# Gathering the experts' rows in quarters and turning them on VectorE, in a decoder layer with a mixture of experts

## What is computed

```python
def moe_ffn(hn, w_router, b_router, w_gate_up, b_gate_up, w_down, b_down):
    logits = (xt @ w_router).astype(jnp.float32) + b_router.astype(jnp.float32)
    top_vals, top_idx = lax.top_k(logits, TOP_K)
    gates = jax.nn.softmax(top_vals, axis=-1)
    ...
    xs = xt[tok]
    h = lax.ragged_dot(xs, w_gate_up, group_sizes) + b_gate_up[e_sorted]
    glu = jnp.minimum(h[:, ::2], SWIGLU_LIMIT)
    lin = jnp.clip(h[:, 1::2], -SWIGLU_LIMIT, SWIGLU_LIMIT)
    act = glu * jax.nn.sigmoid(SWIGLU_ALPHA * glu) * (lin + 1.0)
    y = lax.ragged_dot(act, w_down, group_sizes) + b_down[e_sorted]
    y = y * gates.reshape(-1)[order].astype(y.dtype)[:, None]
    out = jax.ops.segment_sum(y, tok, num_segments=T)
```

## Time and profile before

| | |
|---|---|
| median of 3 runs | 2709.56 us (2707.67 to 2709.72) |
| span of the profiled execution | 2705.4 us |
| instructions | 49571 |
| granted TensorE clock | 0.9 of full speed or more in 38 of 40 slices, 0.8 in two |
| DMA queue q1 (weights, all of SyncE's) | 498.99 MB, 50.2% of 16 engines |

### The profile page before, as it was taken

How to read it: one execution, slowest core, us unless ns; L and a number is a source line. 1 busy time by engine, 2 the same in 40 slices (tenths; PEclk the granted TensorE clock), 3 DMA queues, 4 the chain that set the end, 5 groups by cost and what they waited for, 6 DMA issues and landing times.

```text
span 2705.4 us, 49571 instructions
## 1 busy us (share of the span) xinstructions
PE 2638.0 (98%) x17206; PEld 2118.7 (78%) x17207; DVE 1091.5 (40%) x2701; ACT 627.4 (23%) x1386; POOL 379.9 (14%) x391
## 2 busy tenths in 40 slices
PE   9999999999999998999999999999999999999997
PEld 8455556666477774999999999998878787878785
DVE  1111145554212324433333344344455454545455
ACT  0333355553011112011111111111212121221212
POOL 0100022221000001111111111111111111112111
PEclk9999999999999998999999999999999999999998
DMA  8111243232300002765667677787888888888885
GB/s 293 47 51 54 64 151 90 79 116 92 129 1 9 31 31 103 303 209 194 221 218 254 225 276 260 269 274 264 318 299 319 301 310 306 312 297 312 300 310 202
DMA packets 108856, 533.95 MB, mean 197 GB/s; under 512 B 24290, under 2 KB 59042, under 8 KB 84208
## 3 DMA queue, kind: packets, MB, share of 16 engines
q1 hardware_dynamic: 88016, 498.99, 50.2%
q0 software_dynamic: 20768, 33.97, 5.7%
HBM read 506.64 MB, written 60.52 MB: 210 GB/s over the span
## 4 chain that ended last, share of the span: by engine, by line
PE 92%; DVE 3%; issue 2%; DMA 2%; ACT 1%; DVEq 1%; POOL 0%; ACTq 0%; POOLq 0%
PE bank L1376 45%; PE wide L1376 9%; PE wide L1836 9%; PE wide L1804 9%; PE bank L1426 8%; PE bank L1369 4%; PE wide L1500 2%; PE bank L1556 2%; PE bank L1760 2%; PE wide L1517 1%; DMA d_sum<-y_sb,sidx 1%; PE wide L1369 1%; DVE biased L2060 1%; DVE prob_t L2071 1%; ACT prob L1151 0%
## 5 line engine op out<-in xcount | busy, mean ns | idle before, releaser
L1376 PE MATMUL bank<-xe_t,slot 128*128 128x128 f32 (+4 forms) x8192 | 1025.2, 287 | 12.3 <-issue 11.2
L1376 PEld LDWEIGHTS bank<-xe_t,slot 128*128 128x128 f32 x8192 | 1014.5, 192 | 14.1 <-issue 13.7
L2336 DVE TENSOR_SCALAR glu<-bank,b_gu 128x256 f32<-128x256 f32 x256 | 123.8, 484 | 657.2 <-PE bank L1376 657.1
L1317 ACT ACTIVATE sig<-glu 128x256 f32<-128x256 f32 x256 | 106.7, 417 | 837.8 <-DVE glu L2336 835.5
L1836 PE MATMUL wide<-slot,act_t 128*128 128x512 f32 x608 | 267.8, 593 | 1.0 <-DVE act_t L2348 1.0
L1804 PE MATMUL wide<-act_t,slot 128*128 128x144 f32 (+3 forms) x1664 | 235.5, 302 | 0.0
L1804 PEld LDWEIGHTS wide<-act_t,slot 128*128 128x128 f32 x1664 | 231.8, 190 | 0.0
L1426 PE MATMUL bank<-w_in,xt 128*128 128x512 f32 (+1 forms) x512 | 217.6, 575 | 1.6 <-DVEq L1978 1.6
L1836 PEld LDWEIGHTS wide<-slot,act_t 128*128 128x128 f32 x608 | 112.5, 190 | 128.8 <-issue 126.2
L1334 ACT ACTIVATE y_t<-wide,b_dn 128x256 f32<-128x256 f32 x248 | 102.0, 471 | 421.2 <-PE wide L1836 212.9
L955 POOL DMA_INDIRECT xg<-d_xn,gidx x66 | 66.6, 1009 | 862.8 <-DVE gidx L2290 814.0
(11 more groups left out here) (302 smaller groups left out, 2455.6 us busy)
## 6 DMA issues: line engine op xcount, KB each, us to landing
slot<-in_w_gu SPq DMA_DIRECT2D x128, 2048.0 KB, 8.8
slot<-in_w_dn SPq DMA_DIRECT2D x64, 2048.0 KB, 7.7
w_in<-in_w_in SPq DMA_DIRECT2D x1, 6144.0 KB, 25.3
w_mem_k<-in_w_mem_kv SPq DMA_DIRECT2D x4, 1024.0 KB, 11.0
w_mem_v<-in_w_mem_kv SPq DMA_DIRECT2D x1, 4096.0 KB, 20.6
x_sb<-in_x SPq DMA_DIRECT2D x8, 512.0 KB, 3.3
cneg<-d_cneg SPq DMA_DIRECT2D x8, 512.0 KB, 6.6
d_vw<-mix_out SPq DMA_DIRECT2D x16, 256.0 KB, 2.2
```

The source lines that it names most:

```text
L1317: ac.activation(sig[m % 2][:, :], glu[m % 2][:, :], ACT.Sigmoid, scale=1.702).then_inc(e_sig, 1)
L1376: m = pe.matmul(dst, l, r_, start=(k == 0), stop=(k == n - 1))
L2336: ve.tensor_scalar(glu[b][:, :], pp[b][:, 0:CAP], b_gu[:, bass.ds(e * 2 * KD + 2 * m, 1)], 7.0, ALU.add, ALU.min).then_inc(e_glu, 1)
```

## The change

The gathered rows come to VectorE in such a form that two transposes of 32 x 32 blocks each finish the job, and TensorE turns rows only for the first expert.

- The normed rows are also written to a second table, `d_xq`, with the gain multiplied in (GpSimd, `r_gain`, one product of 128 x 1024 a tile) and each row cut into four interleaved quarters of 1 KB: quarter q holds features 32q to 32q + 31 of each 128. SyncE stores it (`store_quarters`). There is one buffer, `rq`, for all tiles. The gain is brought into row form through a small table `d_g`.
- For every expert but the first, eight indirect DMAs of 128 quarters each replace the two of rows. Partition group q (32 partitions) fetches quarter q, and gather g of a half brings tokens 32g to 32g + 31. The token numbers reach all four partition groups by one more small product (`e_spread`, two bf16 matmuls of 8 columns, after m = 3), and VectorE turns them into indices after its m = 3 (`spread_indices`).
- VectorE's `rows_turned` waits for each half's four gathers and writes `xe_t` directly.
- In GpSimd's queue the scatter of expert i - 1 is issued ahead of the gathers; the wait for its landing and the count in `e_left` stay behind them.
- The one-hots of the first expert and the first weight load wait until the last quarter has been stored.

Cut to its core:

```diff
+        xg_q = nc.alloc_sbuf_tensor_at("xg_q", [P, 2, G32, KD * 32], F32, offset=r.at - 2 * D * 4)
...
+        g_row = Region(59, 63)("g_row", [P, D])
+        rq = Region(55, 59)("rq", [P, G32, KD, 32])
...
+        d_xq = scratch("d_xq", [T * G32, D // G32])
+        d_g = scratch("d_g", [1, D])
...
+            sp.dma_start(d_g[0, :].rearrange("(k p) -> k p", k=KD), a["gains"][:, 3 * KD:4 * KD].rearrange("p k -> k p"),
+                         allow_slow_non_contiguous=True).then_inc(g_row_in, 16)
             sp.wait_ge(c_sum, 1)
+            sp.wait_ge(g_row_in, g_row_in_done + 16)
+            load(g_row[:, :], d_g[0].partition_broadcast(P), g_row_in)
             load(w_xq[:, :, :], rows(a["w_xq"][0]), ld["w_xq"])
...
+            def store_quarters(t):
+                sp.wait_ge(r_rq, r_rq_done + t + 1)
+                sp.dma_start(d_xq[t * P * G32:(t + 1) * P * G32, :].rearrange("(p q) c -> p (q c)", q=G32),
+                             rq.rearrange("p q k d -> p (q k d)")).then_inc(r_stq, 16)
...
             for t in range(NT):
                 if t >= 2:
                     store_rows(t - 2)
+                if t >= 3:
+                    store_quarters(t - 3)
                 if t == NT - 1:
                     store_rows(NT - 2)
+                    store_quarters(NT - 3)
                 sp.wait_ge(x_h, t + 1)
                 if t == NT - 1:
                     store_rows(NT - 1)
+                    for u in range(NT - 2, NT):
+                        store_quarters(u)
                 sp.dma_start(d_sum[t * P:(t + 1) * P, :], h_res[:, t, :]).then_inc(s_st, 16)
...
             sp.wait_ge(r_st, 16 * NT)
+            sp.wait_ge(r_stq, r_stq_done + 16 * NT)
...
+            def r_gain(i):
+                po.wait_ge(r_rn, i + 1)
+                po.wait_ge(r_stq, r_stq_done + 16 * i)
+                apart(po)
+                po.tensor_tensor(rq.rearrange("p q k d -> p k q d"),
+                                 rn[:, bass.ds(i, 1), :].rearrange("p o (k q d) -> p (o k) q d", k=KD, q=G32),
+                                 g_row.rearrange("p (k q d) -> p k q d", k=KD, q=G32), ALU.mult).then_inc(r_rq, 1)
...
                 r_power(i - 1)
+                r_gain(i - 2)
             for t in range(NT - 2, NT):
                 r_rows(t - 2)
                 r_power(t - 1)
+                r_gain(t - 2)
             r_rows(NT - 2)
+            r_gain(NT - 2)
             r_power(NT - 1)
+            r_gain(NT - 1)
...
+            def gather(i):
+                po.wait_ge(e_idx, i + 1)
+                apart(po)
+                for hb in range(2):
+                    for g in range(G32):
+                        n = hb * G32 + g
+                        po.indirect_dma_start(
+                            out=xg_q[:, hb, g, :], out_offset=None, in_=d_xq,
+                            in_offset=bass.IndirectOffsetOnAxis(ap=gidx[:, n:n + 1], axis=0),
+                            bounds_check=T * G32 - 1, oob_is_err=False).then_inc(e_xg[hb], 16)
...
+            def scattered(i):
                 po.wait_ge(e_y.free, 32 * (i + 1))
                 po.sem_inc(e_left, 1)
...
             with po.Fori(1, E) as i:
                 shares(i - 1)
+                scatter(i - 1)
                 gather(i + 1)
-                scatter(i - 1)
+                scattered(i - 1)
...
+            def e_spread(i):
+                pe.wait_ge(e_pt[0].free, spread_use(i))
+                product(pt[0][:, 8:8 + 2 * G32],
+                        [(spread_r.rearrange("p q d -> p (q d)"), ixm[:, c, :, :].rearrange("p h g -> p (h g)"))
+                         for c in range(2)]).then_inc(e_pt[0].full, 1)
...
-                e_gate_up(i, 3, 8, w)
-                e_turn_in(i + 1, (0, 1), later)
+                e_gate_up(i, 3, 4, w)
+                e_spread(i + 1)
+                e_gate_up(i, 4, 8, w)
                 if w == P:
-                    e_rows_down(i, lambda: e_turn_in(i + 1, (2, 3), later))
+                    e_rows_down(i)
                     look_ahead()
                     return
                 e_down_first(i, w)
-                e_turn_in(i + 1, (2, 3), later)
...
+            ve.tensor_reduce(group_r[:, :], ident.rearrange("p (g d) -> p g d", g=G32), AX, ALU.add)
+            ve.tensor_reduce(col_r[:, :], ident.rearrange("p (g d) -> p d g", g=G32), AX, ALU.add)
+            ve.drain()
+            ve.tensor_copy(spread_r[:, :, :], col_r[:, :].unsqueeze(1).to_broadcast([P, G32, 32]))
+            ve.tensor_scalar(quarter_w[:, 0:1], group_r[:, 2:3], 2.0, group_r[:, 1:2], ALU.mult, ALU.add)
+            ve.drain()
+            ve.tensor_scalar(quarter_w[:, 1:2], group_r[:, 3:4], 3.0, quarter_w[:, 0:1], ALU.mult, ALU.add)
+            ve.drain()
+            ve.tensor_scalar(quarter_r[:, :], quarter_w[:, 1:2], float(8 * T * G32), None, ALU.add)
...
+                if not first_one:
+                    x = ve.tensor_tensor(ixm[:, :, :, :],
+                                         pt[0][:, 0:4].rearrange("p (h c) -> p c h", h=2).unsqueeze(3)
+                                         .to_broadcast([P, 2, 2, G32]),
+                                         group_r[:, :].unsqueeze(1).unsqueeze(1).to_broadcast([P, 2, 2, G32]), ALU.mult)
+                x.then_inc(e_pt[0].free, 1)
                 ve.drain()
...
+            def spread_indices(i):
+                ve.wait_ge(e_pt[0].full, spread_use(i))
+                ve.tensor_scalar(gidx[:, :], pt[0][:, 8:8 + 2 * G32], float(G32), quarter_r[:, :], ALU.mult, ALU.add)\
+                    .then_inc(e_pt[0].free, 1)
+                ve.drain().then_inc(e_idx, 1)
...
+            def rows_turned(i):
+                for hb in range(2):
+                    ve.wait_ge(e_xg[hb], rows_landed(i))
+                    ve.transpose(xe_t[:, :, hb * P:(hb + 1) * P].rearrange("p k (g t) -> p k g t", g=G32),
+                                 xg_q[:, hb, :, :].rearrange("p g (k d) -> p k g d", k=KD))
+                ve.drain().then_inc(e_xt, 1)
...
+            ve.wait_ge(r_stq, r_stq_done + 16 * NT)
             hots(0, first)
...
                     if m == 1:
                         indices(i + 1, follow)
+                    if m == 3:
+                        spread_indices(i + 1)
...
-                if last:
-                    x_copies(i + 1, (0, 1))
-                else:
-                    x_copies(i + 1)
+                if not last:
+                    rows_turned(i + 1)
                     hots(i + 2, nxt)
```

More of the change, by code:

```diff
@@ L447, in index_use, with spread_use, turn_in_use, rows_landed @@
         def index_use(i):
-            return e_pt[0].base + 3 * i + 1
-        def turn_in_use(b, i, k):
-            return e_pt[b].base + (3 * i + 1 + k if b == 0 else 2 * i + k)
+            return e_pt[0].base + (1 if isinstance(i, int) and i == 0 else 2 * i + 2)
+        def spread_use(i):
+            return e_pt[0].base + 2 * i + 3
+        def turn_in_use(b, k):
+            return e_pt[b].base + (1 + k if b == 0 else k)
+        def rows_landed(i):
+            return 16 + 16 * G32 * i
         def rows_use(b, i, k, beyond=False):
@@ L574, in build @@
         e_idx = sem("e_idx")
-        e_xg = sem("e_xg")
+        e_xg = [sem(f"e_xg{hb}") for hb in range(2)]
+        g_row_in, g_row_in_done = ld["rope"], 32
+        r_rq, r_rq_done = a_lss, NT
+        r_stq, r_stq_done = a_lrstd, NT
         e_y = Handoff(sem, "e_y")
@@ L1004, in _ @@
             po.sem_inc(e_left, 1)
+            po.wait_ge(r_stq, r_stq_done + 16 * NT)
             gather(1)
@@ L1909, in item @@
                 with pe.If_lt(at, 1):
-                    e_turn_in(0, range(4))
+                    first_turn_in()
                 whole(i, i - 1, w, n_before, later, look_ahead)
```

64 lines of the change are left out of this document (35 added, 29 removed).

## The result

The changed kernel took **2775.59 us**, median of 4 runs (2774.97 to 2778.86), beside 2708.61 (2707.07 to 2709.72) for the kernel before on the same chip: a ratio of **1.0251, 95% interval 1.0239 to 1.0264**. Forecast were 2683 us, and faster. The profiled execution spans 2777.1 us, 71.7 more than before.

A forecast was written before the change was run, and what follows sets the result against it. The prediction took TensorE's own instructions in the expert stage as the bound. Its terms, -35.0 for transposes, +2.9 at the start and +5.4 at the end, sum to -26.7 us: 2683 us, range 2673 to 2703.

The forecast's parts named there:

- the steps: Expert loop: 35.0 us off, 0.8 us in each of 19 steps of 128 columns and 1.67 in each of 12 others.
- the start: Start of the expert stage: the last tile's quarter stores delay the first one-hots, +2.9 us; bounds 2.0 and 5.
- the end: Last step: the later reload of the sums delays ScalarE's squares and VectorE's norm, +5.4 us; bounds 3 and 9.
- hidden behind the first rows' gather: Start of the stage: bias loads and first weight slot move back as much on SyncE, without further cost.
- With the count behind eight gathers, at 28.5 from the step's start: Last step: GpSimd counts the scatter done only behind all eight gathers, so SyncE reloads the sums 9.0 us later.
- the wait that moves: Each step: VectorE's m = 7 waits for the scatter's count behind eight gathers; hidden with 2.7 us to spare, otherwise 0.8.
- Rival 1: Gathers land too late for the next expert's first matmul in the 128-column steps: +34, 2744 us; chance 0.10.
- rival 2: DMA engines are the bound, 128-column steps stay at 43.95 and only the others gain: -11.7, 2698 us; chance 0.08.
- rival 4: End nearly absorbed, as the loads land in 2 us without the weight stream: -33, 2677 us; chance 0.10.
- rival 3: End or start cost more than summed, by slow loads or late row copies: about -15, 2695 us; chance 0.06.
- What bounds the kernel now: Expert stage: TensorE covers 98% of the span, waits at most 11.2 us; each transpose removed saves 0.11 us.
- Transposes out of TensorE: Expert loop: 352 transposes, 38.3 us, leave TensorE; less 0.9 for the last step and 2.4 for added matmuls: 35.0 off.

The follow-up runs named there:

- e12: The changed kernel word for word, measured again on another occasion: 2680.33 us, ratio 0.9895.
- e10: The changed kernel with a drain of GpSimd behind each gather: 3324.45 us, ratio 1.2269.
- e5: The kernel before, with six more gathers without rows a step, issued straight behind the two scatters: 2706.37 us, ratio 0.9991.
- e1: The changed kernel with every loop step's eight gathers left out, VectorE turning a constant instead: 2680.69 us, ratio 0.9902.
- e11: The changed kernel with the wait for the scatters' landing and the count of e_left between the sixth and seventh gather: 2680.44 us.
- e18: The changed kernel with three orders: steps 1-19 as changed, 20-25 e_left counted first, 26-31 four gathers, wait, four gathers: 2739.97 us, ratio 1.0123.
- e13: The changed kernel word for word, measured a third time in another job: 2745.53 us, ratio 1.0140.
- e4: The kernel before, with six more gathers without rows a step, behind the wait for the scatters' landing: 2710.96 us, ratio 1.0008.

## Why the prediction was wrong

**The sum was near where there are no stops.** e12's execution, term by term against the forecast: the steps -32.3 us (from the first step's first matmul to the last step's 1522.2 for 1554.5; forecast -35.0), the start +7.2 (forecast +2.9), the end 0.0 (forecast +5.4). Together -25.2 for -26.7 forecast, a span of 2680.2 and a median of 2680.33 for 2683. That the total came within 2 us is luck in part: three terms were mis-sized, two one way and one the other, and cancelled.

- *The steps*, 2.7 us short. The 128-column steps gained 0.74 us each (0.8 forecast). In e12 the granted clock was 0.50 in three stretches of steps 4 to 13, 13.6 us in all (from 1368.6, 1535.9 and 1839.7), and in the execution before in two of 3.4 (from 1237.4 and 1541.1). At half pace the difference costs an estimated 3.4 us, enough for the shortfall; the prediction had no term for it.
- *The start.* Timeline of the changed kernel (first measurement) at the stage's start, against the earlier trace rows:

```profile
1072.01 2.34 POOL L977 TENSOR_TENSOR rq<-rn,g_row 128x1024 f32<-128x1024 f32 x1 [5.44 <-DMA d_xq<-rq]
...
1078.27 2.67 DVE L2360 TENSOR_SCALAR hot<-const,shift,key 128x256 bf16<-128x256 f32 x8 [1.90 <-issue]
...
1079.22 0.35 SPq L623 DMA_DIRECT2D slot<-in_w_gu  x1
...
1084.84 0.99 POOL L1006 DMA_INDIRECT xg<-d_xn,gidx  x1 [0.30 <-issue]
1094.06 3.84 PE L1834 MATMUL bank<-const,xg 128*128 128x128 f32 x16 [9.48 <-issue]
```

  The one-hots came 4.4 us later (3.4 in e12, 2.9 forecast). What failed here is "hidden behind the first rows' gather": the first rows landed 9.2 us after the second gather's issue where they took 5.1 (9.1 in e12), so another 4 us. The 2 MB weight load, which stood 6.8 us ahead of that gather before, now stands 5.6 ahead of it, and the landing comes 14.8 us after the load's issue (11.9 before). That they wait behind that load was not tried.

- *The end.* "With the count behind eight gathers, at 28.5 from the step's start" failed. e12's last step starts at 2619.9:

```profile
2641.05 1.00 POOL L1018 DMA_INDIRECT xg_q<-d_xq,gidx  x1 [0.30 <-issue]
2641.86 4.27 SPq L623 DMA_DIRECT2D h_out<-d_sum  x8
2642.35 1.00 POOL L1018 DMA_INDIRECT xg_q<-d_xq,gidx  x1 [0.30 <-issue]
...
2655.54 4.10 DVE L2533 SCALAR_TENSOR_TENSOR h_out<-h_out,rstd_f,g_fin 128x1024 f32<-128x1024 f32 x3
```

  SyncE reloads the sums at 2641.86, 21.9 us after the step's start, while five of the eight gathers are still to run. GpSimd's sequencer hands the gathers to its own queue and goes on to the wait and the count without them; what stands behind them in the program does not stand behind their work. The norm starts 35.6 us after the step's start, 35.5 before. For the same reason "the wait that moves" never moved, except in e10. The prediction named this among its signs of being wrong, a reload as far from the last step's start as before: it was at 20.0, and is at 21.9. (From its own 28.5 the reload would be at 2673.6, not 2674.1; half a microsecond of the +5.4.) That the first measurement's end shows just the forecast's +5.4 is chance: its last step has the stops too (granted clock 0.50 for 3.4 us from 2741.4), and e12's end shows nothing.

The other terms held: gathers from 18.3 to 27.8 (18.4 to 27.5), 16 transposes of gathered rows left, and no input for which TensorE waited, in any kernel with the eight gathers but e10. One count was off without effect: the software queue has 23840 packets for 20768, 3072 more in the whole program, where the prediction took 384 more for each expert of 128 rows; its share of the engines' span is 5.7% in both. Rival 1 (gathers land too late) and rival 2 (DMA engines the bound) happened nowhere. The end was absorbed, as in rival 4, but by the early count and not by faster loads, and the start cost more than summed, as in rival 3.

**What failed in the recorded measurement** is the step under "What bounds the kernel now" from TensorE's waits before to "nothing but TensorE's own instructions sets the pace, and an instruction taken from it shortens the stage, as long as nothing else becomes late", and with it the largest term of the sum. "Transposes out of TensorE", put at -35.0, came out at +58.0 between the first step and the last, where it was -32.3 in e12. What the runs show in its place is a wait that the prediction has no rival for: with the gathers beside m = 4 to 7, TensorE's completions come late and it stands without a named releaser (55.4 us in 96 places), and its clock falls behind that. Among the signs of being wrong the only wait was one for VectorE's transpose. Nothing in the trace of before shows it, since the gathers there run from 11.0 to 13.3 us and are two, and e5 shows that merely adding gathers without rows to that kernel does not show it either (on a chip where the changed kernel, run later, had no stops). e1 to e11 say nothing on the cause: they ran where the changed kernel is clean, or was not run beside them.

**What stays open.** What sets an occasion with stops apart: two of four with the changed kernel had them, and the one of e18. The two without stops were on chips that never showed any, one of them met on two occasions; those with stops whose chip is on record (e13, e18) were on two others. No chip is known to have been met twice with stops, so the runs don't part the chip from the loading of the programs. Also open is which mechanism makes TensorE's completions come to light late once the gathers have begun, and whether fewer gathers, or 4 KB ones at that place, are free of it there. One reading is that the DMA engines starve TensorE of instructions. The Trainium skill ("DMA: Bandwidth & Descriptors", Queues, rings and completion order) says that an engine takes its queues in turn, a packet at a time, and handfuls of matmuls 0.7 us apart would suit that; but the Trainium skill ("Runtime: NRT & Kernel Launch", Instruction fetch mechanics) has the fetch run ahead and hidden. The first measurement's profile does record transfers on two instruction queues, the last before the final step at 1886 us; from 1903 to 2711 us, the steps that lose most, the view of DMA queues has none. And a lack of instructions would not by itself make the signal of a finished product late. It was argued, not shown.

The changed kernel was better than the one before on two occasions of four, by 1.0%, and worse on two, by 1.4 and 2.5%. No version that was run is known to beat the kernel before everywhere; where there are no stops the variants, e10 apart, lie within 0.1% of the changed kernel.

## What to carry to other kernels

Measure a change of a few per cent on several occasions before explaining it, and put the kernel in question beside every experiment, or both orders in one program as e18 does. On GpSimd, work that is queued does not delay the semaphore operations behind it in the program, and a drain between queued DMAs costs several microseconds each. And where a rearrangement puts many gathers beside a stretch of short TensorE instructions, read not only TensorE's busy share but when the engine behind it is released.

## What the runs showed that was not expected

- One program, 2679.1 to 2775.6 us by occasion, each steady within 0.3%; the kernel before within 0.05% on the same four.
- VectorE's release by a finished TensorE product up to 6.8 us behind the end of its record (2381.8 and 2388.64), while the records themselves run on at full pace; 0.15 us where nothing is late.
- The first late release ahead of the first packet of the gathers' rows (e18, step 23).
- Behind stops that cost 2.5 us a step the clock fell to 0.50 for 3.4 us in some steps and not in others: 1.7 us more where it did.
- Gathers for which all 128 row numbers are out of bounds cost GpSimd the same 1.0 us each, and six more of them a step cost the kernel before nothing (e4, e5).
